# Attention on one NeuronCore: the exponential over both halves of the queries as one ACT instruction

## The reference

```python
def block_attention(q, k, v):
    ...
        s = jnp.einsum('bqhd,bkhd->bhqk', qi, k).astype(jnp.float32) * ATTN_SCALE
        p = jax.nn.softmax(s, axis=-1)
        return jnp.einsum('bhqk,bkhd->bqhd', p.astype(v.dtype), v)
```

## Time and profile before

| | |
|---|---|
| median of 3 runs | 1501.81 us (1500.98, 1501.81, 1511.92) |
| the profiled execution | 1502.52 us, its span 1500.4 us |
| PE busy | 1395.9 us, 93% |
| DVE busy | 690.5 us, 46% |
| ACT busy | 413.0 us, 28% |
| POOL busy | 217.0 us, 14% |
| mean granted clock of TensorE | 0.961 |

### The profile page before, as it was taken

How to read it: one execution, slowest core, us unless ns; L and a number is a source line. 1 busy time by engine, 2 the same in 40 slices (tenths; PEclk the granted TensorE clock), 3 DMA queues, 4 the chain that set the end, 5 groups by cost and what they waited for, 6 DMA issues and landing times.

```text
span 1500.4 us, 17818 instructions
## 1 busy us (share of the span) xinstructions
PE 1395.9 (93%) x6912; PEld 1085.7 (72%) x6912; DVE 690.5 (46%) x938; ACT 413.0 (28%) x737; POOL 217.0 (14%) x163
## 2 busy tenths in 40 slices
PE   6698999999999988898888988999999999999997
PEld 2697999999943456654454544688889999998786
DVE  5611414232334697667876666654422222223643
ACT  2622211121212122243333332445431111112321
POOL 2310000000023000054434434500000000000000
PEclk9798999999989999999999998999999999999999
DMA  8401333333330021300000000122310001003411
GB/s 366 130 2 33 115 120 138 125 113 120 135 115 11 28 92 65 132 6 6 18 9 0 21 0 16 64 72 95 114 33 30 30 30 30 30 30 108 173 43 56
DMA packets 29918, 107.01 MB, mean 71 GB/s; under 512 B 3659, under 2 KB 7951, under 8 KB 26416
## 3 DMA queue, kind: packets, MB, share of 16 engines
q1 hardware_dynamic: 28144, 99.30, 18.6%
q10 hardware_dynamic: 1728, 7.08, 1.2%
HBM read 89.67 MB, written 16.66 MB: 71 GB/s over the span
## 4 chain that ended last, share of the span: by engine, by line
PE 77%; DVE 11%; issue 4%; DMA 3%; POOL 2%; ACT 1%; SPq 0%; DVEq 0%; PEld 0%; POOLq 0%; ACTq 0%; PEldq 0%
PE bank L538 41%; PE bank L972 13%; PE bank L860 5%; PE bank L888 3%; PE bank L846 3%; PE bank L761 2%; PE bank L1039 2%; DMA SCR<-x_sample_in 2%; DVE SCR L1658 1%; POOL fw L1917 1%; PE bank L825 1%; DVE amax_part L1686 1%; DVE SCR L1716 1%; PE bank L697 1%; PE bank L549 1%
## 5 line engine op out<-in xcount | busy, mean ns | idle before, releaser
L538 PE MATMUL bank<-H_r,WR_r 128*128 128x384 f32 x1728 | 352.8, 336 | 1.4 <-DVE H_r L1811 1.2
L538 PEld LDWEIGHTS bank<-H_r,WR_r 128*128 128x128 f32 x1728 | 302.6, 188 | 6.2 <-issue 4.2
L538 PE MATMUL bank<-H_r,SCR_r 128*128 128x384 f32 x480 | 161.5, 337 | 0.0
L1917 POOL TENSOR_TENSOR fw<-fw,SCR 128x1024 f32<-128x1024 f32 x56 | 133.1, 2377 | 124.3 <-ACT SCR L1322 123.3
L1322 ACT ACTIVATE SCR<-bank 128x512 f32<-128x512 f32 x144 | 83.7, 597 | 160.0 <-PE bank L860 140.3
L1881 POOL TENSOR_SCALAR ssq<-ssq 128x1 f32<-128x1 f32 (+1 forms) x36 | 16.1, 446 | 619.3 <-ACT bank L1067 520.3
L538 PE MATMUL bank<-H_r,WX_r 128*128 128x384 f32 x384 | 100.8, 344 | 3.3 <-PEq L637 3.3
L972 PE MATMUL bank<-H_r,WR_r 128*128 128x512 f32 x432 | 99.9, 394 | 3.8 <-DVE SCR L1844 3.8
L972 PEld LDWEIGHTS bank<-H_r,WR_r 128*128 128x128 f32 x432 | 82.2, 190 | 21.3 <-DVE SCR L1844 4.0
L1482 DVE SCALAR_TENSOR_TENSOR SCR<-bank,col,SCR 128x766 f32<-128x766 f32 (+1 forms) x96 | 43.0, 510 | 108.8 <-ACT SCR L1207 107.3
L538 PEld LDWEIGHTS bank<-H_r,SCR_r 128*128 128x128 f32 x480 | 91.0, 190 | 0.0
(11 more groups left out here) (281 smaller groups left out, 2160.1 us busy)
## 6 DMA issues: line engine op xcount, KB each, us to landing
WR<-w_mod_in SPq DMA_DIRECT2D x16, 1024.0 KB, 7.0
SCR<-w_in_in SPq DMA_DIRECT2D x20, 512.0 KB, 3.4
H<-w_mod_in SPq DMA_DIRECT2D x4, 2048.0 KB, 14.3
SCR<-x_sample_in SPq DMA_DIRECT2D x16, 512.0 KB, 15.3
WR<-w_io_in SPq DMA_DIRECT2D x16, 512.0 KB, 3.4
sp_rows<-SCR SPq DMA_DIRECT2D x9, 512.0 KB, 2.6
KV<-sp_rows SPq DMA_DIRECT2D x9, 512.0 KB, 7.6
H<-w_oe_in SPq DMA_DIRECT2D x2, 2048.0 KB, 13.0
```

The source lines that it names most:

```text
L538: last = nc.tensor.matmul(out, l, r, start=(n == 0), stop=(n == len(pairs) - 1))
L1917: ptt(p_acc, pT[0] if kt == 1 else p_acc, pT[kt % 3], ALU.add).then_inc(p_added, 1)
```

## The change

`exps` issues one activation over both banks, 1024 columns, in place of two of 512. It waits for the scores of both halves, and the semaphore `st_exp` rises by two at its end. What waits for `st_exp` is not edited.

```diff
             def exps(i, s, kt):
 
-                for half in range(2):
-                    act.wait_ge(st_mm, at(i, s, UNITS, unit(kt, half) + 1))
-                    if half == 0:
-                        act.wait_ge(pv_mm, at(i, s, KT9, kt + 1))
-                        act.wait_ge(p_added, at(i, s, KT9 - 1, kt + (kt < 4)))
-                    nc.scalar.activation(pT[kt % 3][:, 512 * half:512 * (half + 1)], bank[:, half, :], ACT.Exp, scale=SCALE).then_inc(st_exp, 1)
+                act.wait_ge(st_mm, at(i, s, UNITS, unit(kt, 1) + 1))
+                act.wait_ge(pv_mm, at(i, s, KT9, kt + 1))
+                act.wait_ge(p_added, at(i, s, KT9 - 1, kt + (kt < 4)))
+                nc.scalar.activation(split(pT[kt % 3], 2), bank[:, 0:2, :], ACT.Exp, scale=SCALE).then_inc(st_exp, 2)
```

## The result

The changed kernel takes 1521.45 us (median of 8 runs, 1517.66 to 1523.51) against 1501.74 for the kernel before; the ratio is 1.0117, with a 95% interval of 1.0093 to 1.0142 (the ratios in this document are estimated from all the runs, so they are not quite the quotients of the medians). 1520 was forecast. The profiled execution took 1519.84 us, with a span of 1517.7; its mean granted clock is 0.953 against 0.961.

The account below looks back on a forecast made before the run. The path was taken to run exponential, POOL add, DVE, PE. Profiled 1502.5 + 11.9 (looped heads 9.2, head 0 0.9, last head 1.8) + 6.4 for clock falls = 1520.8, less 0.7: 1520 us, range 1506 to 1530.

Parts of the forecast that it names:

- ACT's 12 us buy nothing: On ACT, the joined exponentials make it 12 us less busy; it is idle most of the head, so 0 gained.
- The exponential ends 0.57 later: In looped heads, one 1.02 us exponential starts 0.18 after both halves' scores and ends 0.57 later than the pair.
- Four holds: In each looped head, four DVE instructions end behind POOL's later adds: 1.53 us a head, 9.2 for six.
- PE's cover at tile 3: In looped heads only outputs(0) stands between, so scores 3, waiting for the whole exponential, begin 0.37 us later.
- Head 0, 0.9: Head 0 has the first holds but no reciprocal and no L1725: 0.9 us, between 0.4 and 1.3.
- Last head, 1.8: In the last head PE and ACT in turn replace POOL's 2.61 pace with 2.82 to 2.84 a tile: 1.8 us.
- Two more falls of the clock, 6.4: Behind the idle time before max 8, two more heads see the clock fall, 3.2 us each: 6.4 us.
- A: Rival: the clock stays as it is, the holds alone add 11.9 us, about 1514; chance 0.25.
- B: Rival: the clock falls in nearly every head, five more falls at 3.2 us, about 1530; chance 0.13.
- C: Rival: the delay is met once a head and absorbed after the first hold, 1508; chance 0.14.
- Rival D: Adds so late that DVE goes first and two instructions are not held: faster, about 1499; chance 0.05.

Follow-up runs that it names:

- thin_pair: Kernel before (two exponentials), with POOL's add of the probabilities over 8 of the 1024 columns: 1477.3 us, 0.9818.
- thin_one: Changed kernel (one exponential), with POOL's add of the probabilities over 8 of the 1024 columns: 1480.85 us, 0.9853 to the kernel before.
- late_add2: Kernel before, with a 128-column constant add into a spare tile ahead of each POOL add in the looped heads: 1508.08 us, 1.0026.
- los_pair: Kernel before, with DVE's three query lows of a head moved behind the last reduction of its maxima: 1502.00 us, 0.9998.
- late_pair: Kernel before, two exponentials, but the first waits for the scores of both halves: 1516.14 us, 1.0078.
- fill_one: Changed kernel, with twelve unused 128-column matmuls on PE ahead of max 8 in the looped heads: 1521.28 us, 1.0091 to the kernel before.
- one_ends: Kernel before, with one exponential only in heads 0 and 7: 1504.84 us, 1.0009.
- the first order: Kernel before, with DVE's three query lows, L1680 and L1725 all moved behind the last reduction: 1509.78 us, 1.0050.
- late_add: Kernel before, with an 8-column constant add into a spare tile ahead of each POOL add in the looped heads: 1498.87 us, 0.9973.

## Why the prediction was right

- **ACT's 12 us buy nothing.** Right: ACT is 10 us less busy, and no stretch got shorter by it.
- **The exponential ends 0.57 later.** It is 0.63: it starts 0.24 behind the scores, not 0.18. Both forms have the same three waits ahead of the first instruction, and where the 0.06 comes from is not shown. Its length, 1.02, was right.
- **Four holds, 1.53 a looped head.** Right to 0.04 in the two heads where the clock does nothing new (1.53, 1.49), and step by step: against the head's first add, 0.37 had been worked out for the third add, 0.96 for the fifth and 0.96 for the sixth, and head 3 shows 0.38, 1.05 and 0.93. thin_pair and thin_one show that it takes the adds: without them the changed kernel's looped heads are as long as the others to 0.1 us. late_add2 shows it with late adds and nothing else, 1.1 and 0.95 for 1.2. That the other four heads carry the same 1.5 under their falls is an assumption. los_pair, where moving the lows gained less than half of what the holds had promised, does not fit as well.
- **PE's cover at tile 3**, 0.37. Scores 3 begin 0.39 later, and the cover counts through the third add: late_pair, which keeps the cover, has heads 0.6 shorter, and thin_one, which loses it, has hardly longer ones.
- **Head 0, 0.9**: 1.27; the cause of the difference was not looked for. **Last head, 1.8**: 1.45, and 0.46 ahead of its first add, counted in head 6; the pace of 2.83 was right.
- **Two more falls of the clock, 6.4.** The number came out, 7.0, and that is luck. The term was two falls at max 8, each with 6.8 us at the low clock and 3.2 us of cost. What came was three at max 8, two of them half as long, and four behind max 0, a place that the prediction does not name; 23.9 us more at the low clock cost 7.0. Heads 3 and 5 have none of them, though PE idles there as it does in the others, so which heads have one could not be worked out. The changed kernel's runs spread over 6 us.
- **Rivals.** A, the holds without new falls, has 11.9 of the 18.9. B, five more falls at max 8 at 3.2 us each, did not happen: three came, and they cost less. C did not happen: no later hold was absorbed in heads 3 and 5.
- **Rival D**, DVE first, did not happen. Its rule works both ways though: an instruction that was ahead of its add before, L1680, fell behind it in late_pair, fill_one and one_ends, about 2 us each time. This place had been left out of the working; in the profiled execution of the changed kernel it was not held.

## What to carry to other kernels

An engine with idle time isn't free of charge: ask when its result is ready, who starts on it, and what that one shuts out. Joining two short instructions into one saved 0.17 us on the engine here and gave up the overlap of the first with the making of the second's data; the end that others wait for moved by 0.63 us, about the length of one of the two. And a chain of "ends a fixed time after another engine's instruction" in the timeline is a reason to test whether the two share something: taking the other's work away ended it here. Moving such work was worth 0.7% (0.4 to 1.0), but only in an order that minds what is queued behind its result; the first order cost 0.5%. And to compare two runs of a loop, compare trips with the same time at the low clock.

## What was not expected of the hardware

- A third place for falls of the clock: behind max 0, after PE had idled 0.31 ahead of scores 3 and 1.21 ahead of max 0. The same two idle times (0.31 and 1.21 to 1.22) have no fall behind them in heads 3 and 5. In head 2 the outputs that follow it take 1.96 us [the timeline after] in place of 1.08.
- L1680, a copy from SBUF to SBUF with one input, is held by an add as well: 2.32 to 2.66 us in place of 0.48. The Trainium skill (SBUF — State Buffer, "Who interferes with whom") says so of copies that run in a two-port mode; by that rule the traces agree, and what mode this copy runs in no run here shows.
- A kernel that is slower by 0.15 us a head can be faster by 3 us in all (late_add): head 6, without its fall of the clock, is 3.1 us shorter.
